# Gated delta heads: conv 3 ahead of the scaled keys and queries on VectorE, output scaling on ScalarE

## What is computed

```python
q, k, v = split(silu(centred_dwconv(p, conv_w)))         # 5 taps per channel
q, k = l2_norm(q), l2_norm(k)                            # 8 heads, each for 2 value heads
decay = exp(where(lower, gc_i - gc_j, -inf))
a = where(strict, (k * beta) @ k.T * decay, 0)           # per chunk
t_inv = inverse(eye + a)
for chunk in chunks:                                     # forwards, and backwards on flipped tokens
    v_new = u_i - w_i @ s
    o = qd_i @ s + qk_i @ v_new
    s = s * gl_i + kd_i.T @ v_new
o = o_forward + o_backward
y = (rms_norm(o, o_norm_g) * silu(z)) @ w_out            # rms_norm: o * (mean(o*o) + eps) ** -0.5
```

## Time and profile before

| | us |
|---|---|
| median of 3 runs | 2775.22 |
| lowest, highest | 2774.98, 2782.2 |
| profiled execution, its own time | 2771.29 |
| its span in the profile | 2769.6 |
| TensorE, VectorE, ScalarE, GpSimd busy | 2234.2, 1200.7, 548.4, 127.9 |
| the eight delta passes in the trace | about 184 to 992 |

### The profile page before, as it was taken

One profiled execution on the slowest core, in us unless ns is written; L12 is line 12 of the kernel. 1 busy time (PEld: TensorE's weight loads), 2 busy tenths in 40 slices (PEclk: granted clock), 3 DMA queues, 4 the chain that ended last, 5 costly groups with the idle time before them and its releaser, 6 DMA issues. The chain is left out here.

```text
span 2769.6 us, 39984 instructions
## 1 busy us (share of the span) xinstructions
PE 2234.2 (81%) x16012; PEld 1683.0 (61%) x16012; DVE 1200.7 (43%) x2260; ACT 548.4 (20%) x1196; POOL 127.9 (5%) x89
## 2 busy tenths in 40 slices
PE   4489889889889769596667885887888577888997
PEld 1356666656666634173356663877875466777886
DVE  2355665665665610312423785442452454421101
ACT  0034334333344310001201222001001311100000
POOL 0000000000000000000000000000000122100000
PEclk8599999999999989797788995988999787899998
DMA  6110110110110021440022211000002211133443
GB/s 267 65 47 1 47 48 1 47 47 1 47 47 1 2 91 61 182 156 0 0 102 91 92 61 50 1 24 24 1 23 76 80 46 58 64 127 120 153 175 124
DMA packets 50329, 183.58 MB, mean 66 GB/s; under 512 B 5744, under 2 KB 7152, under 8 KB 49648
## 3 DMA queue, kind: packets, MB, share of 16 engines
q1 hardware_dynamic: 50160, 181.18, 17.6%
HBM read 180.11 MB, written 1.05 MB: 65 GB/s over the span
## 5 line engine op out<-in xcount | busy, mean ns | idle before, releaser
L347 PE MATMUL banks<-u,w_ring 128*128 128x256 f32 x1664 | 379.4, 387 | 13.5 <-PEq L190 13.5
L699 PE MATMUL banks<-u,w_ring 128*128 128x512 f32 x768 | 356.0, 601 | 14.0 <-PEq L190 14.0
L347 PEld LDWEIGHTS banks<-u,w_ring 128*128 128x128 f32 x1664 | 319.1, 195 | 60.4 <-issue 17.8
L699 PEld LDWEIGHTS banks<-u,w_ring 128*128 128x128 f32 x768 | 141.2, 192 | 144.7 <-issue 141.6
L484 PE MATMUL banks<-u,w_ring 128*128 128x256 f32 (+1 forms) x640 | 159.5, 413 | 23.4 <-PEq L190 21.0
L484 PEld LDWEIGHTS banks<-u,w_ring 128*128 128x128 f32 x640 | 126.1, 198 | 56.3 <-issue 39.7
L484 PE MATMUL banks<-gated,w_ring 128*128 128x512 f32 (+1 forms) x384 | 139.6, 526 | 11.5 <-PEq L2279 10.0
L484 PEld LDWEIGHTS banks<-gated,w_ring 128*128 128x128 f32 x384 | 73.4, 192 | 77.2 <-issue 74.0
L726 DVE SCALAR_TENSOR_TENSOR acc<-raw,hc,acc 128x512 f32<-128x512 f32 x128 | 96.2, 752 | 4.5
L484 PE MATMUL banks<-ffn,w_ring 128*128 128x256 f32 x352 | 77.9, 385 | 3.0 <-PEq L190 3.0
L426 ACT ACTIVATE sq<-h 128x256 f32<-128x256 f32 (+1 forms) x48 | 18.8, 472 | 304.3 <-PEq L190 304.3
(11 more groups left out here) (467 smaller groups left out, 3720.9 us busy)
## 6 DMA issues: line engine op xcount, KB each, us to landing
w_ring<-in_w SPq DMA_DIRECT2D x323, 512.0 KB, 6.1
h<-in_h SPq DMA_DIRECT2D x2, 2048.0 KB, 7.8
const_base<-in_const SPq DMA_DIRECT2D x1, 1216.0 KB, 9.9
const_part<-in_const SPq DMA_DIRECT2D x1, 1024.0 KB, 5.0
out<-u SPq DMA_DIRECT2D x1, 1024.0 KB, 4.8
const_part<-in_const SPq DMA_DIRECT2D x1, 640.0 KB, 4.4
const_part<-in_const SPq DMA_DIRECT2D x1, 512.0 KB, 3.5
w_rows<-in_rows SPq DMA_DIRECT2D x1, 512.0 KB, 5.6
```

The source lines that it names most:

```text
L347: last = nc.tensor.matmul(out, lhs[k], rhs[k], start=(k == 0), stop=(k == n - 1))
L699: mm = nc.tensor.matmul(self.places[m % len(self.places)][:, :], st.slot(m)[:, P * k:P * k + P], u[:, k, :], start=(k == 0), stop=(k == KT ...
```

## The change

VectorE: `front.conv(3)` and `front.scaled` move ahead of silu 2 and of the mean of squares; before, they stood behind them, with `scaled` ahead of `conv(3)`. GpSimd no longer multiplies `od`; it only takes the roots. ScalarE waits for the root of the outputs' mean behind the decays of chain 3 and then multiplies `od` in place by its eight columns, one 128x128 part per instruction, with the signal `o_norm` on the last; the gates of the next head come behind that. Pass 8 does the same without front work.

```diff
@@ -896,8 +896,6 @@   (GpSimd)
                     if more:
                         front.root(pool)
                     inverse_root(nc, pool, C, ms[:, :], s["o_mean"], s["o_root"])
-                    o3 = od[:, 0, :, :].rearrange("p t (j e) -> p (t j) e", j=2)
-                    link(nc.gpsimd.tensor_tensor(o3, o3, ms[:, :].unsqueeze(2).to_broadcast([P, 2 * TT, P]), ALU.mult), s["o_norm"])
                     if not more:
                         link(nc.gpsimd.memset(lower[:, :, :, half(0)], 0.0))
@@ -1120,6 +1118,13 @@   (ScalarE)
                         front.decays(act, link, 2)
                         front.tanh(act, link, 3)
                         front.decays(act, link, 3)
+                    act.wait_ge(s["o_root"], 1)
+                    for t in range(TT):
+                        for j in range(2):
+                            out = od[:, 0, t, P * j:P * j + P]
+                            link(nc.scalar.activation(out, out, ACT.Copy, scale=ms[:, 2 * t + j:2 * t + j + 1]),
+                                 s["o_norm"] if t == TT - 1 and j else None)
+                    if more:
                         act.wait_ge(s["z_ready"], 1)
                         front.gate(act, link, 0)
                         front.gate(act, link, 1)
@@ -1187,13 +1192,13 @@   (VectorE)
                         front.mean(dve, link)
                     link(nc.vector.tensor_tensor(od[:, 0, :, :], od[:, 0, :, :], od[:, 1, :, :], ALU.add), s["o_sum"])
                     if more:
+                        front.conv(dve, link, 3)
+                        front.scaled(dve, link)
                         front.silu(dve, link, 2)
                     dve.wait_ge(s["o_sqd"], 1)
                     link(nc.vector.tensor_reduce(ms[:, :], o_sq.rearrange("p (a e) -> p a e", e=P), AX.X, ALU.add))
                     link(nc.vector.tensor_scalar(ms[:, :], ms[:, :], 1.0 / P, EPS, ALU.mult, ALU.add), s["o_mean"])
                     if more:
-                        front.scaled(dve, link)
-                        front.conv(dve, link, 3)
                         for c in range(4):
                             front.chain(dve, link, c)
                         front.silu(dve, link, 3)
```

## The result

The changed kernel takes 2798.66 us, the median of six runs, against 2775.10 us before: a ratio of 1.0081, 95% interval 1.0061 to 1.0100. Slower, by 17 to 28 us. A second set of runs beside the experiments gives 2797.18 against 2776.25 us, ratio 1.0063 (1.0043 to 1.0084). The profiled execution took 2802.70 us with a span of 2801.0; the forecast was 2800.7.

A forecast was written before the change was run, and what follows sets the result against it. Two chains, TensorE-ScalarE-VectorE and VectorE's own queue, were taken to bound each pass's end; 7 x 3.42 (2.41 scaling, 1.01 port) + 1.53 = 25.5 us, giving 2800.7 us, range 2785 to 2808.

The forecast's parts named there:

- What bounds the end of a pass: End of each pass: TensorE-ScalarE-VectorE chain and VectorE's own queue end together, so filling holes of 0.53 and 1.24 us gains nothing.
- The rival by which VectorE's queue alone counts: End of a pass: VectorE's queue the only bound, 2.64 us a pass gained, 2756.7 us; chance 0.04.
- The scaling on ScalarE: Behind the last decays: eight copies take 3.43 us, transposes and gated wait; 2.41 us a pass, 1.53 in the last.
- The port: VectorE-GpSimd port: conv 3's first operation held up by the keys' root, making everything behind qn 1.01 us late.
- the upper of two bounds: Conv 3's first operation shut out until GpSimd's root ends, 1.01 us a pass; the lower bound was 0.
- The sum: Whole kernel: seven passes plus the last add 18.4 us without port cost, 25.5 us with it.
- Rival 1: Conv 3 beside the keys' root: no port cost, 2793.6 us; chance 0.34.
- The clock: TensorE's output transposes: idle wait of 5.6 us lowers the clock, so they take 1.94 us instead of 1.04.
- Rival 2: Transposes in TensorE's pause hold its clock up, saving 0.90 there and 1.59 us next pass; 2774 us, chance 0.10.

The follow-up runs named there:

- order_only: Kernel before with only VectorE's new order, output scaling still on GpSimd: 2774.71 against 2776.25 us, ratio 0.9993.
- scale_only: Changed kernel with VectorE's old order restored, so only the scaling moves to ScalarE: 2794.35 against 2776.25 us for the kernel before, ratio 1.0052.
- no_scale: Changed kernel with the output scaling left out, TensorE waiting for the root instead: 2773.97 against 2776.25 us for the kernel before, ratio 0.9990.
- the probe: Changed kernel with conv 3's first operation done five times over, same result each time: 2808.04 us in a single execution.
- the fills: Runs with extra unused TensorE products in its idle time, added to the changed kernel or a faster variant: ratios 1.0113, 1.0033 and 0.9952 to the kernel before.
- early_fill: Kernel before plus VectorE's new order, tanh 3 and silu 3 earlier, five unused TensorE products behind the output transposes: 2760.98 against 2773.27 us, ratio 0.9952.
- pe_fill: Changed kernel plus ten unused 128x512 TensorE products before the output transposes: 2810.53 against 2775.19 us for the kernel before, ratio 1.0113.
- pe_fill_six: Changed kernel plus six unused 128x512 TensorE products before the output transposes: 2782.84 against 2773.27 us for the kernel before, ratio 1.0033.

## Why the prediction was right, and where not

*What bounds the end of a pass.* Right. Two chains met there, and filling VectorE's waits brought nothing, shown by order_only (19.92 to 19.94 us a pass, as before) and by the wait of 1.67 us that came up before chain 2. The rival by which VectorE's queue alone counts (17.3 us a pass) is out.

*The scaling on ScalarE.* Right in each term: 0.401 us a copy, 3.44 us for eight (3.43 was worked out), the transposes at 1.94, `gated` 1.46 us behind the last copy (1.48), the pass 2.39 us longer (2.41), pass 8 1.56 us (1.53). scale_only gives the whole of it alone, no_scale takes the whole of it away.

*The port.* Wrong, and this is the step that failed: the forecast took the upper of two bounds, 1.01 us a pass or 7.1 us in all, for conv 3's first operation beside GpSimd's root. The trace has 0.49 us in all seven passes, and so has the probe, 28 times beside a root. The reason given for taking the upper end, that this form uses more of the memory path and the root has yet to write, did not hold. The better guide was the row that concerned the same GpSimd operation (silu 2 beside a root), not the row that concerned the same VectorE operation beside another GpSimd operation. A likely reason is that the root moves little data for its length (16 columns in and out in 1.64 us, where the multiplication moves 1024 in and 1024 out in 1.9); no run varied this, so it is not shown.

*The sum.* Rival 1, no port cost, is what happened: 18.4 us was worked out, 18.34 measured in the ends of the passes. That the median (2798.66) lies nearer to the forecast (2800.7) than to rival 1 (2793.6) is luck: a term of 7.1 us that does not exist stands in the forecast for a scatter of executions that it did not foresee. The two sets of runs give +23.6 and +20.9 us by medians, with intervals of 17 to 28 and 12 to 23; 18.3 lies inside both, 25.5 inside the first only. scale_only, which has the same ends of passes, gives 9 to 20. What the runs leave open is whether a few microseconds beyond the 18.3 are real; the traces show no place for them that stays the same.

*The clock.* Rival 2 did not happen, for the reason given: after 5.6 us of idling the transposes ran at the low level in every pass (1.94 us each time, granted clock 0.50). The mechanism exists, as the fills show, with a smaller price at the end of a pass than the one worked out: 0.52 us, not 0.90, since `gated` waits for the first four transposes only, and the rest runs beside the first `gated`. Where the clock stayed up into the next pass, its first sixteen transposes were 1.7 us shorter; 1.59 had been worked out.

## What to carry to other kernels

Before moving an operation from an engine that nobody waits for to a "faster" one, look at who is last in the queue that it joins: 1.9 us on idle GpSimd cost nothing, 3.4 us at the tail of ScalarE's queue cost 2.4 us a pass because transposes and two more products stood behind it. A hole in an engine's timeline is worth something only if no other chain ends at the same time; here two edits that are each worth nothing were worth 0.8 us a pass together. Where a bound between two engines is taken from rows, look first at the row with the same operation on the engine that blocks: here it gave the right bound, and the row with the same blocked operation the wrong one.

## What the runs showed of the hardware

- A small power operation on GpSimd (128x8, 1.64 us alone) shuts out neither single-input nor two-input operations of VectorE (conv 3 at 0.49 us, silu 2 at 0.69), but is itself held up by one that is already running: 2.67 us when it starts 0.04 us into a 1.23 us sum. A multiplication of 128x1024 on GpSimd shuts `a_t` operations with two SBUF inputs out for 1.5 of its 1.94 us, and conv 3's single-input form for 0.87; yet `qn`, with one input in SBUF and one in a bank of TensorE's, runs beside it undelayed (0.69 us in seven passes of the kernel before). The Trainium skill ("SBUF — State Buffer", section "SBUF: two separate sides") says that the lock on the shared ports is held for the whole instruction; the multiplication agrees (4.59 instead of 3.08 us), the power operation does not (28 operations beside it at 490 ns or less).
- TensorE's clock can be held up across a pause by products that nobody uses. Five such products in its idle time at the end of passes 1 to 7, 4.46 us each time, made the starts of the eight passes 6.8 us shorter (640.7 against 647.5 us in sum, one trace each) and the ends no longer. In early_fill the clock stayed up in all five passes with a pause of 0.53 to 1.12 us behind the products, and in neither of the two with 4.66 us or more. With pauses of 1.8 to 2.3 us (pe_fill and pe_fill_six) it stayed up for some of the passes only: the sixteen transposes took from 1.94 to 3.60 us.
